# Order of emptying PSUM tiles and splitting weight pieces in the trunk of a hybrid decoder step

## What is computed

```python
def token_mix(x, ...):
    z = x @ w_in + b_in                        # 1024 -> u_a 512, u_b 512, gates 2 x 1024
    out_a = pool_mixer(u_a, ...)               # window means - u_a, times w_pool per group, times pool_scale
    out_b = ssm_mixer(u_b, ...)                # S5 scan, gelu, times sigmoid(y @ w_glu + b_glu)
    merged = sigmoid(z_ga) * (out_a @ w_proj_a) + sigmoid(z_gb) * (out_b @ w_proj_b)
    return merged @ w_out

for l in range(2):
    y = layer_norm(ALPHA * y + token_mix(y), ln1)
    f = swiglu(y, ...) if l == 0 else moe_swiglu(y, ...)   # dense 1024 -> 2816; 8 experts, top 2, 3584 wide
    y = layer_norm(ALPHA * y + f, ln2)
```

## Time and profile before

| | |
|---|---|
| median of three runs | 1713.78 us (1713.28 to 1714.87) |
| the profiled execution | 1714.72 us, span 1713.0 us |
| TensorE busy | 1641.1 us, 96% |
| VectorE busy | 1357.7 us, 79% |
| ScalarE busy | 1001.2 us, 58% |
| mean granted TensorE clock | 0.978 |

### The profile page before, as it was taken

The page is one execution under the profiler, slowest core; times in us unless marked ns, Lnnn a source line. Parts: engine busy times, 40 slices in busy tenths (PEclk is TensorE's granted clock), DMA queues, the critical chain, the costliest instruction groups (busy, mean ns, idle before and its releaser), DMA issues.

```text
span 1713.0 us, 25673 instructions
## 1 busy us (share of the span) xinstructions
PE 1641.1 (96%) x9611; PEld 1398.7 (82%) x9611; DVE 1357.7 (79%) x1480; ACT 1001.2 (58%) x923; POOL 59.1 (3%) x84
## 2 busy tenths in 40 slices
PE   7999999999999998999999999999999999999993
PEld 3878889998899797888888888888888888888883
DVE  5836656767676676988988988998988988989985
ACT  1222544443445236777777777777777777777771
POOL 2002000000000202000000000000000000000002
PEclk9999999999999999999999999999999999999997
DMA  6444245555354326999999999998998998998980
GB/s 160 128 135 123 91 143 165 180 160 173 108 158 155 82 74 220 321 376 336 348 376 326 354 373 329 347 376 329 353 371 314 371 368 313 375 372 309 370 331 25
DMA packets 209696, 441.84 MB, mean 258 GB/s; under 512 B 22896, under 2 KB 26912, under 8 KB 209614
## 3 DMA queue, kind: packets, MB, share of 16 engines
q1 hardware_dynamic: 205518, 435.18, 72.4%
q0 software_dynamic: 2048, 4.29, 1.4%
q10 hardware_dynamic: 2064, 1.45, 0.4%
HBM read 437.06 MB, written 1.93 MB: 256 GB/s over the span
## 4 chain that ended last, share of the span: by engine, by line
PE 80%; DVE 10%; issue 4%; ACT 2%; DMA 2%; SPq 1%; POOL 1%; DVEq 0%; ACTq 0%; POOLq 0%
PE bank L1642 77%; PE bank L1645 3%; DVE w_lo L991 2%; DVE piece_lo L991 2%; DVE ssm L991 2%; ACT piece_hi L735 1%; ACT y_hi L925 1%; DMA r_all<-in_b_glu_dram 1%; DMA piece<-in_w_proj_a_dram 1%; DVE r_all L991 0%; DVE wide L1405 0%; DVE ssm L1439 0%; DMA piece<-in_w_ffn_gate_dram 0%; DVE y_lo L1529 0%; DVE scr L991 0%
## 5 line engine op out<-in xcount | busy, mean ns | idle before, releaser
L991 DVE TENSOR_TENSOR w_lo<-weights,w_hi 128x2048 fp32r<-128x2048 f32 x336 | 765.1, 2289 | 98.6 <-ACT w_hi L934 94.7
L934 ACT ACTIVATE w_hi<-weights 128x2048 fp32r<-128x2048 f32 x336 | 644.4, 1920 | 191.3 <-PE bank L1642 191.2
L1642 PE MATMUL bank<-w_hi,xg_hi 128*128 128x512 f32 x896 | 357.4, 399 | 6.5 <-DVE xg_lo L991 5.0
L1642 PE MATMUL bank<-w_hi,xg_lo 128*128 128x512 f32 x896 | 350.6, 391 | 0.0
L1642 PE MATMUL bank<-w_lo,xg_hi 128*128 128x512 f32 x896 | 349.8, 390 | 0.0
L991 DVE TENSOR_TENSOR piece_lo<-piece,piece_hi 128x1024 fp32r<-128x1024 f32 x126 | 150.8, 1221 | 107.5 <-ACT piece_hi L735 104.3
L735 ACT ACTIVATE piece_hi<-piece 128x1024 fp32r<-128x1024 f32 x126 | 129.5, 1054 | 146.5 <-PE bank L1642 111.7
L1642 PEld LDWEIGHTS bank<-w_hi,xg_hi 128*128 128x128 f32 x896 | 168.6, 188 | 45.7 <-issue 6.9
L1642 PEld LDWEIGHTS bank<-w_hi,xg_lo 128*128 128x128 f32 x896 | 168.5, 188 | 36.9
L1642 PEld LDWEIGHTS bank<-w_lo,xg_hi 128*128 128x128 f32 x896 | 168.9, 189 | 32.9
L1642 PE MATMUL bank<-w_hi,hidT_hi 128*128 128x512 f32 x448 | 175.0, 391 | 0.0
(11 more groups left out here) (315 smaller groups left out, 2156.2 us busy)
## 6 DMA issues: line engine op xcount, KB each, us to landing
weights<-in_w_moe_gate_dram SPq DMA_DIRECT2D x112, 1024.0 KB, 7.3
weights<-in_w_moe_up_dram SPq DMA_DIRECT2D x112, 1024.0 KB, 7.3
weights<-in_w_moe_down_dram SPq DMA_DIRECT2D x112, 1024.0 KB, 6.8
piece<-in_w_in_dram SPq DMA_DIRECT2D x48, 512.0 KB, 3.8
piece<-in_w_ffn_gate_dram SPq DMA_DIRECT2D x22, 512.0 KB, 4.6
piece<-in_w_ffn_up_dram SPq DMA_DIRECT2D x22, 512.0 KB, 4.4
piece<-in_w_ffn_down_dram SPq DMA_DIRECT2D x22, 512.0 KB, 3.9
piece<-in_w_out_dram SPq DMA_DIRECT2D x16, 512.0 KB, 4.4
```

The lines of the kernel that those rows point to most:

```text
L934: act.activation(w_hi[s % PAIRS][:, :], ring_slot[:, :], ACT.Copy).then_inc(w_hi_ready, 1)
L991: return dve.tensor_tensor(out, a, b, op)
L1642: signals(pe.matmul(out, lhsT, rhs, start=start, stop=stop, skip_group_check=True), signal)
```

## The change

The edits change only the order of instructions on ScalarE and VectorE; TensorE, GpSimd and SyncE keep theirs.

- ScalarE, pooling mix of both layers: `h0`, `rows`, `mix` and `w1t` tiles are emptied without splitting ahead of them. Three high halves that stood ahead move between the `w1t` copies, one ahead of the second copy of each pair for as long as the limit allows it.
- VectorE, pooling mix: `oa_lo` of all four tiles comes ahead of three low halves; in layer 1 the low halves of the gates are made sure of first.
- VectorE, `residual`: ahead of an addition only pieces of this projection are split (`split_until`), none of the next one.
- VectorE, `residual` with the rebuilt stream: two low halves come ahead of the four additions.
- VectorE, `layer_norm`: one low half ahead of the wait for the mean, one behind the subtraction.

```diff
+    split_until = {key: sum(e[4] for e in plan[:piece_at[last] + 1])
+                   for key, last in [(("out", l), ("out", l, 1, 3)) for l in range(DEPTH)]
+                   + [(("down",), ("down", 1, NFT // 2 - 1))]
+                   + [(("gate", l), ("gate", l, 3, 3)) for l in range(DEPTH)]}
...
             def transposed_w1(l):
                 for r in range(2):
                     for i in range(4):
+                        if i % 2 == 1:
+                            weights_hi(min(n_hi + 1, split_limit["w1t", l, r, i]))
                         act.activation(w1T[r][:, 4 * i:4 * i + 4, :],
-                                       trunk_tile(("w1t", l, r, i))[:, :].rearrange("p (q n) -> p q n", q=4),
+                                       tile_in(act, ("w1t", l, r, i))[:, :].rearrange("p (q n) -> p q n", q=4),
...
-                                   trunk_tile(("h0", l, r))[:, 0:P].rearrange("p (b q) -> p q b", q=NQ),
+                                   tile_in(act, ("h0", l, r))[:, 0:P].rearrange("p (b q) -> p q b", q=NQ),
...
                 rows_in = x_all if key == ("out", 0) else rT
                 if rows_in is rT:
+                    for _ in range(2):
+                        next_lo((*key, 0))
                     for k in range(0, KD, 2):
...
                 for m in range(KD):
-                    dve.scalar_tensor_tensor(out=rT[:, m, :], in0=trunk_tile((*key, m))[:, 0:T], scalar=factor,
+
+                    weights_lo(min(split_limit[(*key, m)], split_until[key]))
+                    dve.scalar_tensor_tensor(out=rT[:, m, :], in0=tile_in(dve, (*key, m))[:, 0:T], scalar=factor,
...
             def layer_norm(l, which):
                 n = 2 * l + which
+                last = ("out", l, KD - 1) if which == 0 else ("down", KD - 1)
+                next_lo(last)
                 mean = tile_in(dve, ("mean", l, which))[:, 0:T].unsqueeze(1).to_broadcast([P, 2, T])
-                wait_emptied(dve, ("out", l, KD - 1) if which == 0 else ("down", KD - 1))
+                wait_emptied(dve, last)
...
+                next_lo(last)
                 var = tile_in(dve, ("var", l, which))[:, 0:T]
...
                 s5_inputs(l, ("gate", l, 8))
+                weights_lo(split_until["gate", l])
                 for g in range(4):
-                    ps = trunk_tile(("mix", l, g))
+                    ps = tile_in(dve, ("mix", l, g))
```

More of the change, by code:

```diff
@@ L800, in mixer @@
                     n = (PSTATE, NDEC)[s]
-                    act.activation(rows[s], trunk_tile(("rows", l, s))[0:n, :], ACT.Copy).then_inc(emptied["a"], 1)
+                    act.activation(rows[s], tile_in(act, ("rows", l, s))[0:n, :], ACT.Copy).then_inc(emptied["a"], 1)
                 for g in range(4):
-                    act.activation(oa_hi[:, g, :], trunk_tile(("mix", l, g))[:, 0:T], ACT.Copy,
+                    act.activation(oa_hi[:, g, :], tile_in(act, ("mix", l, g))[:, 0:T], ACT.Copy,
                                    scale=colD[:, 4 * l + g:4 * l + g + 1]).then_inc(oa_hi_ready, 1)
```

## The result

| | before | after |
|---|---|---|
| median of five runs | 1713.28 us (1708.54 to 1714.87) | 1698.73 us (1693.0 to 1702.23) |
| profiled execution, its span | 1714.72, 1713.0 us | 1702.23, 1700.1 us |
| mean granted TensorE clock in it | 0.978 | 0.981 |

The ratio is 0.9914 (95% interval 0.9896 to 0.9932), a gain of 14.7 us with an interval of 11.7 to 17.8. Forecast were 1701.2 us and 1697.5 to 1706.5. Between the two profiled executions the span fell by 12.9 us; the sum of the prediction was 12.6.

The account below looks back on a forecast made before the run. The prediction took the chain of waits, on TensorE for 80% of the span, as the bound. Its terms -6.0 - 1.4 - 4.4 + 0.4 - 0.6 - 0.6 = -12.6 gave 1701.2 us, range 1697.5 to 1706.5.

Parts of the forecast that it names:

- The mix of layer 0: Layer 0's pooling mix: ScalarE's copies no longer wait behind high halves, chunk products start at 127.6, not 133.61: -6.0 us.
- Rival (a): Layer 0's mix: fourth piece's landing doesn't follow TensorE, ScalarE stands at its high half; -3.2 not -6.0, 1704.0 us; chance 0.12.
- The mix of layer 1: Layer 1's pooling mix: first pieces already landed, chunk products start at 552.0 instead of 553.43: -1.4 us.
- Layer 0's projection and LayerNorm: Layer 0's output projection and LayerNorm: tiles no longer queue behind a late feed-forward half, next step at 232.3: -4.4 us.
- Rival (b): Layer 0's LayerNorm: wait only moves, VectorE waits for the half between last tile and subtraction; 1705.6 us; chance 0.07.
- The down LayerNorm: Down projection's LayerNorm: the half between last tile and subtraction outlasts the wait there: +0.4 us (0 to +1.2).
- The starts: Starts of down projection and layer 1's output projection: low halves come ahead of additions, TensorE waits less: -0.6 us each.
- Rival (d): SyncE's DMA issues behind late low halves: each microsecond over the up projection's 9 us cover is lost; 1719 us; chance 0.02.

Follow-up runs that it names:

- fill kernel: The kernel before with 14 products of the identity ahead of layer 0's fourth mix tile, filling TensorE's idle: ratio 1.0021 (with 28 products 1.0018).
- mix_act: The kernel before with ScalarE's new order in the pooling mixes alone, VectorE keeping its old order: ratio 1.0027, +4.6 us.
- norm_only: The kernel before with only the new places of the low halves in residual and layer_norm, without the two ahead of the four additions: ratio 0.9969, -5.3 us.

## Why the prediction was right

**The mix of layer 0**, forecast -6.0 (-3.2 to -6.7): the step is -6.44 in the pair of traces and -5.4 between the averages of five traces each. ScalarE went as worked out: last copy ended at 127.46 (127.5 forecast), chunk products at 127.52 (127.6). That these times agree to 0.1 is in part luck: `h0` stood 0.34 later than before, and from `h0` on the stage took 10.48 where 127.6 - 116.70 = 10.9 was forecast, 0.4 less, as in layer 1. The piece was issued 120.22 - 119.91 = 0.31 after the first transpose and its half began at 124.88 without an idle, as forecast for 125.0: the release moved with the transpose. Rival (a), with the fourth piece, didn't come true. A small form of it, with the third piece, shows in two of the five traces of the new order (0.49 and 0.90, above) and cost 0.6 and 1.0 us there. The prediction asked only whether the fourth piece lands in time.

**The mix of layer 1**, forecast -1.4, came to -1.83. Three small sizes make the 0.4: ScalarE began its copies 0.58 after TensorE's `h0` transposes (531.39 against 530.81), where 541.8 was 0.7 after theirs; the copies down to `oa_hi` took 2.99 and not 3.11; and the `w1t` copies with the three halves 6.86 and not 7.0.

**Layer 0's projection and LayerNorm**, forecast -4.4: -4.18. The subtraction follows the last tile by 220.90 - 219.42 = 1.48, where 226.4 - 224.9 = 1.5 was worked out. Rival (b) fell in two kernels. But the -4.18 isn't the idle alone: part of it is the clock's. At the mean the step is -3.34; from the mean to 232.37 another -0.84 comes. Before, the mean ran in the stretch of low clock at 228.46, VectorE waited 1.90 for it, and from the last tile to the subtraction it took 230.50 - 228.18 = 2.32 where layer 1 takes 1.23. So some 1.1 us of the gain are the full clock's, less 0.25 for the half that comes ahead of the subtraction now. The prediction had these 1.1 us in its -4.4, because it took layer 1's stage as the undisturbed one, but it named the clock only at the mix.

**The down LayerNorm**, forecast +0.4: +0.24, from 436.09 to 443.45, 7.36 us against 7.12. VectorE starts the half 0.08 before the tile's end and the subtraction 0.09 before the half's, which back-to-back rows show and my sum left out.

**The starts**, forecast -0.6 each: at down the idle fell from 2.04 to 1.42, -0.62; layer 1's step is -0.70.

**The sum's remainder.** In the pair of traces the clock cancels: the stretch at 402.54 has gone (it makes up 1.57 of the -2.19 of the down stage), the one near 480 is twice as long (the +1.56 ahead of layer 1's `h0`). Windows of after, then of before at the same two places of the program:

```profile
478.59:485.42 6.83, 6.83 (x32) 6.83 (x33) 5.39 (x10) 1.72 (x5) 0.00 (x0) 0.50 0.35 103
390.83:394.24 3.41, 2.27 (x18) 2.27 (x19) 3.41 (x4) 1.06 (x1) 0.00 (x0) 1.00 0.23 84
```
```profile
490.29:497.12 6.83, 6.83 (x46) 6.83 (x46) 5.94 (x11) 2.66 (x5) 0.00 (x0) 0.75 0.32 94
402.54:405.95 3.41, 3.41 (x15) 3.41 (x16) 3.41 (x5) 0.00 (x0) 0.00 (x0) 0.50 0.56 166
```

Of the two other stretches that went, that at 122.65 lay over a stage that waited for ScalarE; the fill kernel shows that taking it away alone gains nothing there. That at 228.46 did cost, some 1.1 us, as said above. By the ratios the gain is 14.7 and 15.1 us, 2 more than the sum, which lies inside both intervals. The forecast time was 2.5 us above the median of after. It was tied to one profiled execution, and single executions of the same kernel differ by more than that (below).

**Where the reasoning was thin.** The forecast was right by its mechanism. Rival (d) took the cover from the place of a high half in ScalarE's order, 9 us, and the run showed 16. The rival was unlikely either way, but the price was wrong by a step of method. And nothing in the prediction said that the two engines' edits need each other; from its text, which put the gain to ScalarE, one would have forecast a gain for mix_act, as I did, and it loses.

## What to carry to other kernels

Where two engines empty PSUM in turn, look at both orders: here the copies moved ahead on one of them were worth nothing (VectorE) or lost (ScalarE), as long as the other's next tile was still queued behind other work, and only both together gained. Postponed splitting went into waits that exist anyway at little or no cost here (behind the subtraction, behind the last copy), and its latest place is set by when TensorE reads the half, to be taken from TensorE's timeline and not from where the other engine does it now.

## What the runs showed of the hardware

**The spread of single runs goes with the clock.** In 75 executions of the kernel before, the span ran from 1703.1 to 1716.1 us and the mean granted clock from 0.984 to 0.976. The nine executions at 0.984 took 1703.1 to 1707.8, the ten at 0.978 1711.0 to 1714.4; a line through all has -1.2 us for each 0.001, with a correlation of -0.90. A difference between two single traces below 5 us says nothing unless it is taken stage by stage.

**A long idle of TensorE and a stretch at 0.50 go together, a short one leaves it to chance.** Over the 14 traces:

| place | idle of TensorE | traces with a stretch at 0.50 there |
|---|---|---|
| layer 0's transposes | 2.9 to 5.1 us | 6 of 6 |
| the same | none or filled | 0 of 8 |
| layer 0's mean | 2.9 to 4.2 us | 8 of 8 |
| the same | none | 0 of 6 |
| start of down | 2.04 us | 3 of 8 |
| the same | 1.42 us | 0 of 6 |

Two windows over layer 0's mean, before and in norm_only:

```profile
228.46:231.87 3.41, 3.41 (x12) 3.00 (x13) 1.51 (x4) 0.63 (x2) 0.00 (x0) 0.50 0.19 72
```
```profile
221.28:224.69 3.41, 2.95 (x19) 2.28 (x18) 3.21 (x5) 1.00 (x2) 0.00 (x0) 1.00 0.24 37
```

An idle isn't the only thing that such a stretch follows. Before, those at 139.71 and 559.55 stand where TensorE has no idle row. In all 14 traces, in both layers, a stretch at 0.50 of 3.4 to 10.2 us begins in the last half of the chunk products (256 instructions of 32 columns or fewer, behind the transposes and kernel matrices) or within 0.5 us of their end: 28 of 28. Which property of that stage brings it stays open, since no run changes it.
